# The last down step by token halves, and five waits moved, in a one-core decoder block

## What is computed

```python
h = rmsnorm(x, g_pre_mix); proj = h @ w_in            # q, k, v and gate columns of all branches
y_a = nsa_attention(...)   # kc, vc = silu(blocks @ w1) @ w2; compressed, selected and window softmax
y_b = retention(q_r, k_r, v_r) * silu(rg)             # 4 heads
mkv = rmsnorm(mem, g_mem) @ w_mem_kv; y_c = memory_attention(mq, mk, mv)   # 4 heads, 256 memory tokens
merged = gate0 * (y_a @ w_br_nsa) + gate1 * (y_b @ w_br_ret) + gate2 * (y_c @ w_br_mem)
x = x + rmsnorm(merged @ w_o, g_post_mix)
u = causal_dwconv(rmsnorm(x, g_pre_ffn) @ w_up)       # 2 x 5632 columns, width 3
f = (gelu(u_gate) * u_val) @ w_down                   # 5632 -> 2048
return x + rmsnorm(f, g_post_ffn)
```

## Time and profile before

| | us |
|---|---|
| median of 3 runs | 1752.44 (1752.35 to 1752.77) |
| the profiled execution, its own time | 1752.13 |
| its span, from the first to the last instruction | 1749.8 |
| PE busy | 1710.7 |
| DVE busy | 1095.5 |
| ACT busy | 817.0 |
| mean DMA rate | 187 GB/s |

### The profile page before, as it was taken

How to read it: one execution, slowest core, us unless ns; L and a number is a source line. 1 busy time by engine, 2 the same in 40 slices (tenths; PEclk the granted TensorE clock), 3 DMA queues, 4 the chain that set the end, 5 groups by cost and what they waited for, 6 DMA issues and landing times.

```text
span 1749.8 us, 26499 instructions
## 1 busy us (share of the span) xinstructions
PE 1710.7 (98%) x9645; PEld 1499.8 (86%) x9645; DVE 1095.5 (63%) x1426; ACT 817.0 (47%) x1107; POOL 42.9 (2%) x49
## 2 busy tenths in 40 slices
PE   6999999999999999999999999999999999999997
PEld 6998999999878888888888788888888888888885
DVE  5644557666566454564565667776676676676676
ACT  5433335444434434434444555455454455454453
POOL 0000000000031000000000100000000000000000
PEclk9999999999999999999999999999999999999999
DMA  8755458545465666666647555666666666666663
GB/s 260 228 176 185 143 147 275 159 144 156 150 199 165 191 197 192 208 201 193 190 166 252 182 166 188 191 190 187 190 193 192 189 190 188 191 192 191 193 188 115
DMA packets 246146, 327.77 MB, mean 187 GB/s; under 512 B 12727, under 2 KB 167464, under 8 KB 245544
## 3 DMA queue, kind: packets, MB, share of 16 engines
q1 hardware_dynamic: 246056, 326.47, 60.2%
HBM read 321.71 MB, written 3.67 MB: 186 GB/s over the span
## 4 chain that ended last, share of the span: by engine, by line
PE 94%; DVE 2%; DMA 2%; ACT 1%; issue 0%; SPq 0%; DVEq 0%; POOL 0%; ACTq 0%; POOLq 0%
PE bank L1295 18%; PE bank L1285 15%; PE bank L1286 15%; PE bank L1287 15%; PE bank L1299 9%; PE bank L1259 4%; PE bank L1261 4%; PE bank L1260 4%; PE bank L1272 1%; PE bank L1274 1%; PE bank L1273 1%; DMA wraw<-in_w_in 1%; DVE wlo L795 1%; ACT whi L527 1%; DMA wraw<-in_w_o 0%
## 5 line engine op out<-in xcount | busy, mean ns | idle before, releaser
L795 DVE TENSOR_TENSOR wlo<-wraw,whi 128x1024 fp32r<-128x1024 f32 x588 | 722.6, 1234 | 481.5 <-ACT whi L527 479.5
L527 ACT ACTIVATE whi<-wraw 128x1024 fp32r<-128x1024 f32 x588 | 621.4, 1060 | 719.2 <-PE bank L1287 395.0
L1295 PE MATMUL bank<-hx,whi 128*128 128x512 f32 x1376 | 344.5, 392 | 0.0
L1295 PEld LDWEIGHTS bank<-hx,whi 128*128 128x128 f32 x1376 | 248.0, 189 | 44.9
L1299 PEld LDWEIGHTS bank<-hx,wlo 128*128 128x128 f32 x1376 | 187.7, 190 | 13.4
L1299 PE MATMUL bank<-hx,wlo 128*128 128x256 f32 x1376 | 191.9, 282 | 0.0
L1285 PE MATMUL bank<-whi,hx 128*128 128x512 f32 x448 | 175.7, 392 | 0.0
L1287 PE MATMUL bank<-whi,hx 128*128 128x512 f32 x448 | 174.4, 389 | 0.0
L1286 PE MATMUL bank<-wlo,hx 128*128 128x512 f32 x448 | 174.3, 389 | 0.0
L1285 PE MATMUL bank<-whi,r_hi 128*128 128x512 f32 x416 | 162.2, 390 | 0.0
L1286 PE MATMUL bank<-wlo,r_hi 128*128 128x512 f32 x416 | 162.0, 389 | 0.0
(11 more groups left out here) (241 smaller groups left out, 2071.6 us busy)
## 6 DMA issues: line engine op xcount, KB each, us to landing
wraw<-in_w_in SPq DMA_DIRECT2D x200, 512.0 KB, 3.6
wraw<-in_w_up SPq DMA_DIRECT2D x176, 512.0 KB, 4.4
wraw<-in_w_down SPq DMA_DIRECT2D x88, 512.0 KB, 4.2
wraw<-in_w_mem_kv SPq DMA_DIRECT2D x32, 512.0 KB, 4.3
wraw<-in_w_o SPq DMA_DIRECT2D x32, 512.0 KB, 4.4
wraw<-in_w_br_mem SPq DMA_DIRECT2D x16, 512.0 KB, 4.1
wraw<-in_w_br_nsa SPq DMA_DIRECT2D x16, 512.0 KB, 4.5
wraw<-in_w_br_ret SPq DMA_DIRECT2D x16, 512.0 KB, 4.3
```

The lines of the kernel that those rows point to most:

```text
L527: nc.scalar.activation(whi[:, c], wraw[:, c], ACT.Copy).then_inc(hi_done, 1)
L795: V.tensor_tensor(wlo[:, c], wraw[:, c], whi[:, c].bitcast(F32), ALU.subtract).then_inc(lo_done, 1)
L1295: T.matmul(ps[UP_PAIRS[j][t]][:, :], whi[:, c, k, t * P:(t + 1) * P], hx[:, :, k0 + k, :], start=first and k == 0, stop=False, skip_group_ ...
```

## The change

- *Memory scores*: the groups of `mv` swap their bank pairs: the first writes banks 2 and 7 and waits for nothing, the second writes 0 and 1. The scores in bank 2 then wait for the first group's evacuation only.
- *Compression weights early*: the last compression quad is loaded into a part of `arena` that the memory keys have left, four transfers on SP ahead of `mix`, and converted from there; the quad after it is loaded into `wraw` one quad sooner.
- *Sparse scores*: the two waits are left out.
- *Retention*: DVE does the decay product ahead of the first `lo`.
- *Reload of x*: two more quads of `w_o` are loaded ahead of it.
- *Output projection*: chunks 2 and 3 of the quad before the last are also done by token halves. Chunks 2 and 3 of the first quad of `w_up` are therefore converted later, in the middle of the halves' chains. Rows are taken in three parts (1024, 512, 512). POOL clears M after the last `lo` of the normed tiles.
- *Last down step*: all four groups for tokens 0 to 127, then all four for 128 to 255, in eight banks; chunks of the last quad are kept in `m_hi` and `m_lo`. The norm of the first half, its `post` and its stores follow while PE does the second; the second half has four `post` of 512 columns.

The diff, cut to its core (waits and counts that only follow from it are left out):

```diff
@@ -89,19 +89,20 @@
+X2_PARTS = [(0, 1024), (1024, 1536), (1536, 2048)]
-OUT_PARTS = [(0, 0, 512), (0, 512, 1024), (1, 0, 1024), (1, 1024, 512), (0, 1536, 512), (1, 1536, 512)]
+OUT_PARTS = [(0, 0, 1024), (0, 1024, 1024), (1, 0, 512), (1, 512, 512), (1, 1024, 512), (1, 1536, 512)]
-NEW_PAIRS = ("mv", "rg")
+LAST_BANKS = ((0, 1, 6, 7), (2, 3, 4, 5))
...
@@ -227,7 +229,16 @@
-        WO_LAST, UP_FIRST = Q0["wo"] + 7, Q0["up0"]
+        CMP_LAST = Q0["mix"] + 5
+        WO_LAST, UP_FIRST, DN_LAST = Q0["wo"] + 7, Q0["up0"], Q0["dn"] + 1
+        def early(c):
+            return arena[:, A_MK + 1024 * c:A_MK + 1024 * (c + 1)]
+        def kept(buf, c):
+            return (m_hi, m_lo)[buf].rearrange("p k s -> p (k s)")[:, 1024 * c:1024 * (c + 1)]
@@ -354,7 +365,19 @@
+            sp.wait_ge(m_o, MH + 1)
+            for c in range(4):
+                sp.dma_start(early(c).rearrange("p (k n) -> p k n", k=CK), rows(cmp_w1_v, 16 + 4 * c, 0)).then_inc(s_early, 16)
+                if Q0["mix"] + m == CMP_LAST:
+                    continue
+                if Q0["mix"] + m == CMP_LAST + 1:
+                    for c in range(4):
+                        sp.wait_ge(lo_done, 4 * (CMP_LAST - 1) + c + 1)
+                        sp.sem_inc(loaded[c], 16)
+                        sp.dma_start(wraw[:, c], rows(w_in, 4 * c, C_KV + (3 + n) * GW)).then_inc(loaded[c], 16)
+                    continue
@@ -386,9 +409,12 @@
+            for j in range(2):
+                quad(Q0["wo"] + 2 + j, lambda c: rows(w_o, 8 * j + 2 * c, 2 * GW, 2 * GW, 2), lambda c: wide(wraw, c))
-            loop(Q0["wo"] + 2, 3, 2, wide_cols(w_o, 2 * GW), into_wide)
+            loop(Q0["wo"] + 4, 2, 2, wide_cols(w_o, 4 * GW), into_wide)
@@ -505,20 +531,31 @@
             half_rstd(5, 7)
-            pool.wait_ge(s_x2, 2 * TT)
+            pool.wait_ge(s_trl, 2 * KT)
-            rstd(6)
+            half_rstd(6, 0)
+            half_rstd(7, 1)
         @block.scalar
             def hi(q, c):
+                if isinstance(q, int) and q == CMP_LAST:
+                    act.wait_ge(s_early, 64)
+                    act.wait_ge(pe_done, 4 * q + (c - 3))
+                    nc.scalar.activation(whi[:, c].rearrange("p k n -> p (k n)"), early(c), ACT.Copy).then_inc(hi_done, 1)
+                    return
+                    return
+                if isinstance(q, int) and q == DN_LAST:
+                    nc.scalar.activation(kept(0, c), wraw[:, c].rearrange("p k n -> p (k n)"), ACT.Copy).then_inc(hi_done, 1)
...
@@ -694,9 +731,9 @@
             def row_squares(t, h):
-                act.wait_ge(s_x2, 2 * t + h + 1)
-                nc.scalar.activation((r_hi, r_lo)[t][:, 1024 * h:1024 * (h + 1)], X[:, t, 1024 * h:1024 * (h + 1)], ACT.Square,
-                                     accum_out=sq[:, 1, t, h:h + 1]).then_inc(s_ssq, 1)
+                act.wait_ge(s_x2, 3 * t + h + 1)
+                own = slice(*X2_PARTS[h])
+                nc.scalar.activation((r_hi, r_lo)[t][:, own], X[:, t, own], ACT.Square, accum_out=sq[:, 1, t, h:h + 1]).then_inc(s_ssq, 1)
             def half_hi(t, pairs):
@@ -709,14 +746,16 @@
             group_squares(3, 0)
-            row_squares(0, 0)
-            row_squares(0, 1)
+            ahead(WO_LAST, (2, 3))
+            for h in range(3):
+                row_squares(0, h)
+            row_squares(1, 2)
@@ -768,9 +807,9 @@
-            for g in range(4):
-                for t in range(TT):
-                    act.wait_ge(s_dn, 4 + 8 * (STEPS - 1) + 2 * g + t + 1)
+            for t in range(TT):
+                for g in range(4):
+                    act.wait_ge(s_dn, 4 + 8 * (STEPS - 1) + 4 * t + g + 1)
@@ -788,7 +827,13 @@
-                if isinstance(q, int) and q == WO_LAST:
+                if isinstance(q, int) and q == CMP_LAST:
+                    V.tensor_tensor(wlo[:, c].rearrange("p k n -> p (k n)"), early(c), whi[:, c].rearrange("p k n -> p (k n)").bitcast(F32),
+                                    ALU.subtract).then_inc(lo_done, 1)
+                elif isinstance(q, int) and q == DN_LAST:
+                    V.tensor_tensor(kept(1, c), wraw[:, c].rearrange("p k n -> p (k n)"), kept(0, c).bitcast(F32),
+                                    ALU.subtract).then_inc(lo_done, 1)
+                elif isinstance(q, int) and q == WO_LAST:
@@ -876,9 +921,9 @@
-                ch.add(V.tensor_copy(by_head(A_MV + 1024 * i, 0), ps[PAIRS[i][0]][:, :].rearrange("p (h n) -> p h n", h=2)))
-                ch.link(V.tensor_copy(by_head(A_MV + 1024 * i, 1), ps[PAIRS[i][1]][:, :].rearrange("p (h n) -> p h n", h=2)))
-                dve.sem_inc(evac[i], 1)
+                ch.add(V.tensor_copy(by_head(A_MV + 1024 * i, 0), ps[PAIRS[1 - i][0]][:, :].rearrange("p (h n) -> p h n", h=2)))
+                ch.link(V.tensor_copy(by_head(A_MV + 1024 * i, 1), ps[PAIRS[1 - i][1]][:, :].rearrange("p (h n) -> p h n", h=2)))
+                dve.sem_inc(evac[1 - i], 1)
@@ -1006,12 +1051,11 @@
-                    ahead(q, (0,))
                     dve.wait_ge(r_i, r + 1)
-                    ahead(q, (1,))
+                    ahead(q, (0, 1))
                     dve.wait_ge(r_o, r + 1)
...
@@ -1129,10 +1174,11 @@
-            residual(0, 0)
-            residual(0, 1)
-            dve.wait_ge(s_ssq, 2 * 2 * TT + 2)
-            half_square(0, 6, 2, 1)
+            for h in range(3):
+                residual(0, h)
+            ahead(WO_LAST, (2,))
+            dve.wait_ge(s_ssq, 2 * 2 * TT + 3)
+            half_square(0, 6, 3, 1)
@@ -1144,10 +1190,12 @@
             half_lo(0, (2, 3))
+            ahead(WO_LAST, (3,))
+            residual(1, 2)
             half_lo(0, (4, 5))
-            dve.wait_ge(s_ssq, 2 * 2 * TT + 4)
-            half_square(1, 6, 2, 1)
+            dve.wait_ge(s_ssq, 2 * 2 * TT + 6)
+            half_square(1, 6, 3, 1)
             half_lo(0, (6, 7))
@@ -1226,22 +1274,26 @@
             def times_gain(g, t):
-                dve.wait_ge(s_sq, 8 + 2 * g + t + 1)
+                dve.wait_ge(s_sq, 8 + 4 * t + g + 1)
                 f = M[:, t, 512 * g:512 * (g + 1)]
                 ch.add(V.tensor_tensor(f, f, GP[:, 512 * g:512 * (g + 1)], ALU.mult))
-            for g in range(4):
-                if g < 2:
-                    ahead(Q0["dn"], (2 * g, 2 * g + 1))
-                for t in range(TT):
-                    down_group(Q0["dn"], g, t).then_inc(s_dn, 1)
-                if g:
-                    for t in range(TT):
+            ahead(Q0["dn"])
+            for t in range(TT):
+                for g in range(4):
+                    dve.wait_ge(s_dl, 4 * t + g + 1)
+                    f = M[:, t, 512 * g:512 * (g + 1)]
+                    V.tensor_tensor(f, ps[LAST_BANKS[t][g]][:, :], f, ALU.add).then_inc(s_dn, 1)
+                    if g:
-            mean_square(4, 4, (s_sq, 16), lambda: [times_gain(3, t) for t in range(TT)], 6)
-            ch.wait()
-            for part in OUT_PARTS:
-                post(M, *part, s_fin)
+                dve.wait_ge(s_sq, 8 + 4 * t + 4)
+                half_square(t, 0, 4, 0)
+                times_gain(3, t)
+                ch.wait()
+                dve.wait_ge(s_rstd, 7 + t)
+                for part in OUT_PARTS:
+                    if part[0] == t:
+                        post(M, *part, s_fin)
         @block.tensor
...
@@ -1385,14 +1440,20 @@
             def group(q, chunks, i, phase, x_, between={}, tiles_ready=None):
-                for b in range(2):
-                    if b == i % 2 or (i == 0 and phase in NEW_PAIRS):
-                        pe.wait_ge(evac[b], G0[phase] // 2 + i // 2)
+                if phase == "mv":
+                    for b in range(2 * i):
+                        pe.wait_ge(evac[b], G0[phase] // 2)
+                else:
+                    for b in range(2):
+                        if b == i % 2 or (i == 0 and phase == "rg"):
+                            pe.wait_ge(evac[b], G0[phase] // 2 + i // 2)
+                pair = PAIRS[(i + (phase == "mv")) % 2]
-                    chunk_w(q + c // 4, c % 4, PAIRS[i % 2], *x_, 2 * c, c == 0, c == chunks - 1)
+                    chunk_w(q + c // 4, c % 4, pair, *x_, 2 * c, c == 0, c == chunks - 1)
@@ -1479,8 +1540,8 @@
-                            for b in range(2):
-                                pe.wait_ge(evac[b], G0["nq"] // 2)
+                            pe.wait_ge(evac[1], G0["nq"] // 2)
                         for t in range(TT):
@@ -1559,8 +1620,6 @@
                                 pe.wait_ge(s_kce, 1)
-                                for b in range(2):
-                                    pe.wait_ge(evac[b], G0["rqk"] // 2)
@@ -1657,9 +1716,11 @@
             pe.wait_ge(evac[1], G0["wo"] // 2 + 1)
-            for c in range(4):
+            for c in range(2):
             for t in range(TT):
+                for c in range(2, 4):
+                    chunk_w_half(WO_LAST - 1, c, t, PAIRS[1], *MM, 2 * c, False)
@@ -1687,12 +1748,39 @@
```

(26 more changed lines are left out.)

17 lines of the change are left out of this document (11 added, 6 removed).

## The result

The changed kernel takes 1735.91 us (median of four executions, 1735.22 to 1736.51), the one before 1752.61 in the same comparison: a ratio of 0.990, 95% interval 0.9888 to 0.9913. Executed again (`after_again`) it took 1735.79 (1735.6 to 1735.92), ratio 0.9901 (0.9886 to 0.9916). The kernel before was executed 70 more times beside the experiments; their median is 1753.36, 0.9 above the one that I started from.

The account below looks back on a forecast made before the run. PE was taken to bound the kernel (busy 1710.7 of 1749.8 us), so only its standing still and the tail pay; eight gains sum to 14.8 us, giving 1737.6 us for the median, with a range of 1735.5 to 1741.2.

Parts of the forecast that it names:

- Retention: Retention heads: decay product ahead of the first `lo` removes PE's waits; gain 2.4 us, at least 1.5.
- the row + 0.16: PE's listed waits: each costs its length in the profile plus 0.16 us that the modelled matmul end hides.
- The tail: Last matmul to the end: earlier first `post`, four shorter `post`, less to store; gain 3.8 us, between 3.0 and 4.3.
- the memory scores: Memory attention: score matmuls run during the copies instead of behind them; gain 1.65 us, between 1.4 and 1.8.
- compression itself: Compression: early weights remove three waits, 0.35 us of waiting stays; gain 2.25 us, between 1.3 and 2.6.
- Transition: Output projection to `w_up`: halves and the later clearing shorten PE's waits; gain 1.5 us, between 0.3 and 2.5.
- the extra `lo`: Transition, on DVE: a second `lo` (1.14 us) ahead of a `half_lo` uses up the 1.1 us PE gained.
- the late chunk: Last down step: last chunk ready at 1724.4, PE wants it at 1724.6; cost 0, 0.2 us to spare.
- The clearing that holds up the `lo`: Rival, next quad after the transition: POOL's clearing delays the first `lo`, PE waits 3.2 us; 1740.8 us, chance 0.14.
- The last step did not starve: Rival, last down step: late chunk or DVE's order costs PE 2 us in the first half; 1739.6 us, chance 0.07.
- The waits did not only move: Rival, compression and middle chain: gains only 1.3 and 0.3 instead of 2.25 and 1.5; 1739.8 us, chance 0.06.
- the slower rival: Rival, 1020 to 1741 us: without pauses TensorE is granted less clock; at 0.96, 1767 us; chance 0.02.

Follow-up runs that it names:

- undo_compression: Changed kernel with only the early compression weights undone, the last compression quad going through wraw again: 1739.69 us, 3.9 slower.
- b_lo_in_gap: Changed kernel with one `lo`, chunk 3 of the last output projection quad, moved on DVE to directly behind the first diagonal: 1735.53 us.
- undo_last_step: Changed kernel with the last down step, its parts and its stores as before: 1739.66 us, 3.9 slower.
- pool_reads: Changed kernel with a copy on POOL, which reads SBUF, put ahead of the clearing of M: 1740.55 us, 4.8 slower.
- before_look_2: The kernel before, unchanged, profiled once more: 1752.79 us, mean clock 0.996.
- before_look_4: The kernel before, unchanged, profiled once more: 1752.53 us, mean clock 0.997.
- before_again: The kernel before, unchanged, profiled once more: 1753.11 us, mean clock 0.998.

## Why the prediction was right or wrong

Forecast 1737.6, range 1735.5 to 1741.2; measured 1735.9. The direction and the place of every gain were right, and of the cases it was the forecast one that came. What failed is the size: the sum was 1.7 too small, and two of its terms carry that. Retention was put at 2.4 and gave 3.0, because the price of a wait (the row + 0.16) was too low. The tail was put at 3.8 and gave 4.4, because the end was left 3.56 us behind the posts. That the time still lies inside the range, 0.4 from its lower end, is owed to a range that reaches to all gains at their upper ends. The third point below, the clock, is no cause of the 1.7: it lies in the executions of the kernel before, not in those that the forecast started from.

- **The price of a wait.** The rule was the row plus 0.16. Right was about 0.1 more: the memory scores gave 1.85 instead of 1.65 (there the prediction had also taken 0.16 off for a late bank 0, and no wait for it came), the sparse scores 1.2 instead of 1.05, retention 3.0 instead of 2.4. In retention four waits of that price add up, and the fourth, "0.1 to 0.2 below the view", was 0.3. Together 0.9 us.
- **The tail.** "Worked out, the first `post` starts at 1740.0": 3.39 us behind the last matmul; measured 3.35 (the last one starts at 1736.61). The four posts took 2.74, not 2.56. The step that failed is the end, which I left 3.56 behind the posts, with only "a little more" for 1 MB to store instead of 2. Measured, it is 2.7: the tail gave 4.4 instead of 3.8.
- **The clock.** Ahead of the prediction I read PEclk where PE was busiest, found 1.00, and priced waits by PE's time alone. In part of the executions of the kernel before, the compression waits also halve the granted clock behind them for some 3 us, at a price of 1.4 to 1.5. The profile I had was without it, and 1752.44, the median that I set the sum against, was of three executions; that of 70 is 1753.36. So the clock does not move the forecast time, but it adds about 1 us to what the change is worth: the medians differ by 17.6 us (1753.36 - 1735.79), the profiled executions by 16.4 (1752.13 - 1735.69).

Against them stands compression itself: 1.5 and 2.0 instead of 2.25. The waits went as worked out (2.3, and no 0.35 stayed), but 0.3 to 1.0 came back ahead of them, at landings of other chunks: 0.3 of it at the first keys and values, with the early weights and without them (undo_compression waits 0.47 there, and four of the five profiles of the kernel before 0.2 to 0.3; the one that the prediction read has no such wait). The other part came in one of two profiles. No cost of the early transfers themselves shows beyond that.

**Memory values, reload of x**: 1.1 each, as predicted (1.1 and 1.05).

**Transition**: 1.5, and for the reasons given: the diagonal took 0.3, and the three `lo` beside the clearing took their 3.50. But the halves, with which the working began, add only 0.3, and the clearing, undone, takes all 1.5 back. That the extra `lo` uses the 1.1 up was the right sentence, and b_lo_in_gap shows it: moved away, 0.8 comes back.

**Last step**: the late chunk did what was worked out. No PE wait stands in it, and undo_last_step reaches the last matmul no sooner.

**The rivals.** The clearing that holds up the `lo` did not happen; pool_reads shows that it would have, had POOL read. The last step did not starve. The waits did not only move. The clock was not lower without pauses but behind some of them: the slower rival had the sign the wrong way round. (Its 1752 + 14 is 1766, not 1767; nothing hangs on it.)

**What I said the profile would show** came: L1548 at 0.2 (now L1609), diagonal and `lo` as said, no wait in the last 22 us, and 8.4 us from the end of the last matmul, under the 9 forecast. The wait before the first chunk of half 0 grew to 1.34: one of 0.6 stood there before, PE comes 1.7 earlier and gains 1.1 of that, so the working had 1.2.

## What to carry to other kernels

Price a wait of TensorE by what starts late behind it, not by its row, and where several short ones stand close together read the granted clock behind them in more than one profile: removing them may win back a granted clock that the profiled execution never lost. In a chain across engines, look first for the instruction that is held by another engine's (undoing the one moved clearing cost 1.5 us, undoing the rearranged half quad 0.3); then ask of each instruction that is moved into the chain which gap it could fill instead. And work the tail out to the last store, not to the last product: the backlog behind it shrinks with the bytes.

## What the runs showed of the hardware that was not expected

- The granted clock fell to its 1.2 GHz level behind three waits of 0.4, 1.6 and 0.4 us (undo_compression), and behind 0.2, 1.1 and 0.7 (before_look_2), none of them long. Nearly equal waits in another profile of the same kernel (0.28, 1.11 and 0.79 in before_look_4), and 1.44 and 1.09 in before_again, left it at 1.00. What decides between them was not tried.
- A clearing on POOL, which only writes, held up a DVE `tensor_scalar` from SBUF to SBUF (the diagonal, 3.10 instead of 0.28 us), but not three with two SBUF inputs (3.50 beside it and without it), nor a `half_lo` that reads PSUM and one SBUF tensor. A copy on POOL held up the first `lo`, by 3.2 us. SBUF — State Buffer, "Who interferes with whom", of the Trainium skill tells these apart: a `tensor_scalar` can run in a 2-port mode, and for these the page says that they contend with GpSimd, without its exception for one that only writes. The rows agree; that the diagonal runs in that mode no run here shows by itself.
- A power of 128 values on POOL took 0.92 us beside a gain product with two SBUF inputs, 0.54 without one.
